# A ring of gather places that changes its size while the kernel runs

## The reference

```
qh = (x @ w_q).reshape(T, 8, 2, 128)            # 8 heads, two halves
s  = einsum('thcd,hcnd->thcn', qh, keys)        # 128 keys in each half
...                                             # top 16 of the pair sums: 16 experts of 16384 per head
gates = softmax(top_s)
act = gelu(einsum('thkd,td->thk', u[experts], x))
y   = einsum('thk,thkd->td', gates * act, v[experts])
```

## Time and profile before

| | |
|---|---|
| median of 3 runs | 4133.05 us |
| lowest and highest of them | 4130.08 and 5259.92 us |
| the profiled execution's own time | 4129.4 us |
| its span, first to last instruction | 4127.6 us |
| granted TensorE clock, mean | 0.851 |
| busy: PE, DVE, ACT, POOL | 2945.9, 3013.0, 1444.9, 1617.4 us |
| moved by DMA | 1521.92 MB, of that 1366.06 MB on Pool's queue |

### The profile page before, as it was taken

How to read it: one execution, slowest core, us unless ns; L and a number is a source line. 1 busy time by engine, 2 the same in 40 slices (tenths; PEclk the granted TensorE clock), 3 DMA queues, 4 the chain that set the end, 5 groups by cost and what they waited for, 6 DMA issues and landing times.

```text
span 4127.6 us, 32638 instructions
## 1 busy us (share of the span) xinstructions
PE 2945.9 (71%) x9247; PEld 1519.2 (37%) x9247; DVE 3013.0 (73%) x6069; ACT 1444.9 (35%) x4189; POOL 1617.4 (39%) x1309
## 2 busy tenths in 40 slices
PE   6699756875977744767868876776887787665565
PEld 2365342444532311323446323344354633222122
DVE  0406769878898846687778886978787898666666
ACT  1213323532233321335632332542475233332232
POOL 0001332334544424344433553434544354444443
PEclk8798888987999976787879998888988899888888
DMA  8143897989998999899999999999999999999998
GB/s 355 67 166 137 325 391 280 339 333 357 410 396 363 405 408 382 329 402 405 407 387 402 406 382 383 384 417 419 411 410 415 419 417 377 422 421 414 420 421 364
DMA packets 222323, 1521.92 MB, mean 369 GB/s; under 512 B 29757, under 2 KB 33537, under 8 KB 48822
## 3 DMA queue, kind: packets, MB, share of 16 engines
q0 software_dynamic: 186912, 1366.06, 81.5%
q1 hardware_dynamic: 35230, 153.77, 9.4%
HBM read 1516.49 MB, written 3.24 MB: 368 GB/s over the span
## 4 chain that ended last, share of the span: by engine, by line
DMA 31%; PE 28%; DVE 24%; issue 8%; POOL 4%; ACT 4%; DVEq 1%; SPq 1%; PEldq 1%; PEld 0%; ACTq 0%
DMA core_ring<-in_l_uv,core_experts 24%; PE sum_rows L1986 8%; DVE core_ring L1946 7%; DVE core_yv L1961 4%; POOL core_ring L1929 4%; PE sum_rows L2263 2%; PE j_in_ps L490 2%; DMA layer_slot<-in_l_uv,core_experts 1%; PE s1c_query_pq L1700 1%; DMA s0a_h_w<-in_l_peer_wq 1%; PE j_query_pq L1700 1%; DMA mod_w<-in_l_w_mod 1%; PE s1b_in_ps L490 1%; PE s0b_out_po L629 1%; DVEq L159 1%
## 5 line engine op out<-in xcount | busy, mean ns | idle before, releaser
L1929 POOL DMA_INDIRECT core_ring<-in_l_uv,core_experts x1209 | 1521.1, 1258 | 2085.0 <-PE sum_rows L1986 954.8
L1986 PE MATMUL sum_rows<-core_ring,core_diag 128*128 128x512 f32 x2820 | 1540.9, 692 | 596.7 <-ACT core_diag L1975 472.3
L1946 DVE CUSTOM_DVE_ANT_0 core_ring<-core_ring,core_hc 128x1024 f32<-128x1024 f32 x1209 | 1466.8, 1223 | 612.2 <-DMA core_ring<-in_l_uv,core_experts 433.6
L1986 PEld LDWEIGHTS sum_rows<-core_ring,core_diag 128*128 128x128 f32 x2820 | 577.7, 218 | 1482.6 <-ACT core_diag L1975 786.0
L1969 ACT ACTIVATE core_wt<-core_wt 128x1 f32<-128x1 f32 x1280 | 256.4, 200 | 1655.7 <-DVE core_wt L1946 1572.9
L1961 DVE SCALAR_TENSOR_TENSOR core_yv<-core_ring,core_wt,core_yv 128x1024 f32<-128x1024 f32 x494 | 632.8, 1281 | 17.9 <-ACT core_wt L1972 17.3
L1972 ACT ACTIVATE core_wt<-core_wt,core_gates 128x1 f32<-128x1 f32 x1280 | 376.8, 294 | 41.6
L1975 ACT ACTIVATE core_diag<-core_ident,core_wt 128x128 f32<-128x128 f32 x705 | 283.1, 402 | 23.0
L1986 PE MATMUL sum_rows<-layer_slot,layer_diag 128*128 128x512 f32 x184 | 107.7, 716 | 45.6 <-ACT layer_diag L1975 34.8
L2263 PE MATMUL sum_rows<-core_ring 128*128 128x416 f32 x320 | 117.5, 526 | 5.2 <-DVEq L159 4.1
L1946 DVE CUSTOM_DVE_ANT_0 layer_slot<-layer_slot,core_hc 128x1024 f32<-128x1024 f32 x71 | 86.9, 1224 | 40.5 <-DMA layer_slot<-in_l_uv,core_experts 30.5
(11 more groups left out here) (778 smaller groups left out, 3285.6 us busy)
## 6 DMA issues: line engine op xcount, KB each, us to landing
mod_w<-in_l_w_mod SPq DMA_DIRECT2D x16, 2048.0 KB, 11.9
core_ring<-in_l_uv,core_experts POOLq DMA_INDIRECT x1209, 11.9
core_ring<-in_l_w_mod POOLq DMA_DIRECT2D x6, 2048.0 KB, 10.1
s_mix_pr<-in_l_w_in SPq DMA_DIRECT2D x5, 1664.0 KB, 11.2
core_ring<-in_l_w_in POOLq DMA_DIRECT2D x5, 1664.0 KB, 10.5
p_h_w<-in_l_peer_wq SPq DMA_DIRECT2D x16, 512.0 KB, 4.6
s0a_h_w<-in_l_peer_wq SPq DMA_DIRECT2D x16, 512.0 KB, 12.9
s0b_h_w<-in_l_peer_wq SPq DMA_DIRECT2D x16, 512.0 KB, 8.2
```

Of the source, the lines that this page charges most:

```text
L1929: nc.gpsimd.indirect_dma_start(self.slots[r], None, core.a[f"l{layer}_uv"], bass.IndirectOffsetOnAxis(ap=self.experts[:, t, n:n + 1], axis ...
L1946: nc.vector.tensor_tensor_reduce(self.slots[r][:, 0:D], self.slots[r][:, 0:D], self.hc[:], 1.0, 0.0, ALU.mult, ALU.add, self.wt[:, r:r + 1 ...
L1986: mm = nc.tensor.matmul(self.py[:, c * 512:(c + 1) * 512], self.diags[r], self.slots[r][:, D + c * 512:D + (c + 1) * 512], start=(at == 0) ...
```

## The change

The ring's places are no longer worked out by a formula but handed out in turn from a list, `turns`, to which places can be added and from which they can be taken while the program is written out. `place(n)` pops the first of the list, notes it with its count, and puts it back at the end.

- Behind layer 0's mixers two places are opened: one for good (in a stage "late" that lasts to the end) and one in a stage "rest" that lasts over `other_experts` of layer 0 and layer 1's modulation. The second is taken out of the turns ahead of the modulation, which leaves nine.
- Behind layer 1's last attention stage two more are opened in a stage "last", which makes eleven, for what is left to gather then.
- Pool waits before the first gather into such a place until the engines' last meeting before it was opened is over (`free_from`).
- Since the places are known only when everything else is written out, both calls of `bg.gather` move to the end of `program`.
- There are twelve semaphores of each kind and twelve columns of weights (`PLACES`).

```diff
-RINGS = (RING, 9)
+PLACES = 12
...
-        self.used = [new(f"used{r}") for r in range(max(RINGS))]
+        self.used = [new(f"used{r}") for r in range(PLACES)]
...
+        self.turns, self.placed, self.times, self.free_from = list(range(RING)), [], [0] * PLACES, {}
...
-    def more_slots(self, stage):
-        for r in range(RING, RINGS[1]):
+    def open_places(self, stage, count):
+        opened = range(len(self.slots), len(self.slots) + count)
+        for r in opened:
             self.slots.append(stage.sb(f"slot{r}", [P, 2 * D])[:])
             self.diags.append(stage.sb(f"diag{r}", [P, P])[:])
+            self.free_from[r] = 4 * self.core.meetings
+            self.turns.append(r)
+        return opened
+    def close_places(self, places):
+        for r in places:
+            self.turns.remove(r)
     def place(self, n):
-        half = TILES * SLOTS
-        if n < half:
-            return n % RINGS[0], n // RINGS[0]
-        rnd, r = divmod(n - half, RINGS[1])
-        return r, rnd + (half // RINGS[0] if r < RINGS[0] else 0)
+        while len(self.placed) <= n:
+            r = self.turns.pop(0)
+            self.placed.append((r, self.times[r]))
+            self.times[r] += 1
+            self.turns.append(r)
+        return self.placed[n]
...
                     r, rnd = self.place(q * SLOTS + n)
+                    if rnd == 0 and r in self.free_from:
+                        pool.wait_ge(core.meeting, self.free_from[r])
                     pool.wait_ge(self.used[r], rnd + 1)
...
-            for r in range(max(RINGS)):
+            for r in range(PLACES):
                 dve.sem_inc(self.used[r], 1)
...
             early.load()
-            bg.gather(0)
...
-        other_experts(core, "s0b", latents[1:], 0, 1, REST_RATES)
-        with Stage(core, "mod1_c") as m:
-            modulation_stage(core, 1, "mod1", m.sb("silu", [P, DK, 32])[:], early.MOD_CHUNKS, [1, 4], 2, (2.5, PE_0, 3))
-        with Stage(core, "layer1") as last:
-            bg.more_slots(last)
-            bg.gather(1)
+        with Stage(core, "late") as late:
+            bg.open_places(late, 1)
+            with Stage(core, "rest") as rest:
+                more = bg.open_places(rest, 1)
+                other_experts(core, "s0b", latents[1:], 0, 1, REST_RATES)
+                bg.close_places(more)
+                with Stage(core, "mod1_c") as m:
+                    modulation_stage(core, 1, "mod1", m.sb("silu", [P, DK, 32])[:], early.MOD_CHUNKS, [1, 4], 2, (2.5, PE_0, 3))
             with Stage(core, "s1_att") as m:
...
-            other_experts(core, "s1c", latents[2:], 1, 7, LATENT_RATES)
-            stored = store_rows(core)
-            bg.allow(2 * TILES)
-            bg.finish(2 * TILES - 1)
...
+            with Stage(core, "last") as last:
+                bg.open_places(last, 2)
+                other_experts(core, "s1c", latents[2:], 1, 7, LATENT_RATES)
+                stored = store_rows(core)
+                bg.allow(2 * TILES)
+                bg.finish(2 * TILES - 1)
...
+        for layer in range(2):
+            bg.gather(layer)
```

More of the change, by code:

```diff
@@ L1867, in __init__ @@
         self.yv = mem.sb("yv", [P, D])
-        self.wt = mem.sb("wt", [P, max(RINGS)])
+        self.wt = mem.sb("wt", [P, PLACES])
         self.diag = mem.sb("diag", [P, RING, P])
@@ L1876, in __init__ @@
         self.gelu_done, self.wt_done, self.diag_done = new("gelu_done"), new("wt_done"), new("diag_done")
-        self.used = [new(f"used{r}") for r in range(max(RINGS))]
+        self.used = [new(f"used{r}") for r in range(PLACES)]
         self.slots = [self.ring[:, r, :] for r in range(RING)]
         self.diags = [self.diag[:, r, :] for r in range(RING)]
+        self.turns, self.placed, self.times, self.free_from = list(range(RING)), [], [0] * PLACES, {}
         self.order = new("order")
         self.gate_in = new("gate_in")
-        self.row_in = [new(f"row_in{r}") for r in range(max(RINGS))]
+        self.row_in = [new(f"row_in{r}") for r in range(PLACES)]
         self.owners, self.on_pe, self.last_add = [], places_on_pe(4), None
@@ L2496, in program, with _ @@
                 attention_stage(core, "s1c_attend", latents, [2, 3], pr, qT, kT, vc, env["h"], attention, LATENT_RATES["attend"])
-            other_experts(core, "s1c", latents[2:], 1, 7, LATENT_RATES)
-            stored = store_rows(core)
-            bg.allow(2 * TILES)
-            bg.finish(2 * TILES - 1)
-            @core.block.sync
-            def _(sp):
-                sp.wait_ge(stored, 16 * TILES)
+            with Stage(core, "last") as last:
[4 more added lines that the diff above has]
+                bg.finish(2 * TILES - 1)
+                @core.block.sync
+                def _(sp):
+                    sp.wait_ge(stored, 16 * TILES)
+        for layer in range(2):
+            bg.gather(layer)
 def store_rows(core):
```

## The result

Median 4097.52 us (4092.37 to 4099.06, 4 runs) against 4131.57 us before; the ratio is 0.9924, 95% interval 0.9912 to 0.9936. (A slow run of the kernel before, 5259.92 us, is not in the ratio.) That is 0.76% or 31 us less, where 43.6 us were forecast: clear of no change by the interval, though less than two per cent. Measured once more beside another experiment, the ratio was 0.9916 (0.9901 to 0.9931).

What follows compares the result with a forecast made beforehand. After about 900 us transfers were taken to bound the kernel, except where below 422 GB/s. Gains of 19.1, 17.4 and 7.1 us sum to 43.6 us, taken from the median 4133.05: 4089.4 us, range 4045 to 4131.

Steps and rivals of the forecast that it cites:

- The bound and the sign: After about 900 us transfers bound the kernel, except where they fall below 422 GB/s; more places save 43.6 us.
- Emission, 0: Whole program: writing the gathers out last, working out turns while building, and three more semaphores at the start cost 0.
- added waits: Pool's four waits before first gathers into new places: taken as 0, at most 2.48 us each, 10 us in all.
- Two places to 1490, 19.1 us: Gathers of about 905 to 1490 us: two more places shorten four dips by 5.0, 5.0, 5.0 and 4.1 us.
- tile boundary: Dip at 1240 to 1270 us, with Pool's 16.48 us wait: loses 14.4 us, two more places give 5.0.
- One place to 2400, 17.4 us: About 1490 to 2400 us, nine places for eight: seven dips each give one gather's 2.48 us.
- The end, 7.1 us: From 3160 us on, two more places: the dip at 3450 gives 5.0 us, that at 3800 gives 2.1.
- The bounds: Whole gain: at least 18 us by comparing stretches with eight and nine places, at most 130 us, all lost outside 2400 to 3160.
- The limit of seven gathers: Pool's descriptor memory, 1,024 bytes of a partition, holds seven gathers at most; six dips would give 15 us less, sum 29.
- Rival A: In dips foreground matmuls and DVE's order decide; only tile boundaries at 1240 and 3450 give 5.0 us each: 4123 us, chance 0.15.
- Rival B: Nearly all lost bandwidth comes back, also where few gathers are under way: 75 to 130 us saved, say 4030 us; chance 0.09.
- Rival C: In the projections foreground weights come late behind more gathers: at a quarter of 279 us, 26 us slower, 4159; chance 0.06.

Runs made afterwards that it cites:

- the first experiment: The changed kernel's new turns, waits and gathers written last, but the sizes of the kernel before (eight places, nine from gather 640): 4126.2 us, ratio 1.0001 to before.
- the fourth experiment: The kernel before's sizes (eight, then nine places) in the new way of writing out, plus two places at the end, eleven: 4123.46 us, ratio 0.9989 to before.

## Why the prediction came out right, point by point

*The bound and the sign.* Right. The stretch without a new place, 2400 to 3160, took 774 us both times; three of the four with one got shorter, by less waiting at the same busy time of DVE. The sum was too high: 43.6 us against 31. The stretches below are cut at the dot products named above and taken over all profiles with the same places in that stretch; their parts, 14, 10 and 5 us, add up to 29. Of the signs, 905 to 1470 us moved 401 GB/s, as said, and the tail stayed at 422; from 1640 to 2400 it was 391 GB/s and not 398. The range was wide, from 2 to 88 us saved, so that the time fell into it says little by itself.

*Emission, 0.* Right, by the first experiment. The added waits were not tried alone, but none shows in the changed kernel: Pool's first gathers into the new places, at 904.6, 905.8, 3147.8 and 3149.1 us, begin 0.30 us after the issue before them.

*Two places to 1490, 19.1 us.* 16 us between the two profiles; with eight places four profiles take 505 to 509 us from dot product 146 to 320, with ten four take 493 to 495: some 14 us. The term that failed is the 5.0 us for the tile boundary from 1240 to 1270: it gave nothing (14.2 us lost against 14.0). The other three terms came out near their size: ahead of the boundary, where 10.0 us were counted for two dips, 12.5 instead of 22 to 26 us are lost, and behind it 3 us less, where 4.1 were counted. The prediction took four dips as four gains; but at the boundary a new place holds a row that has landed, or one nearly so, and the queue is fed no longer for it. What decides that a row has landed by then is not shown: DVE's waits for rows just before don't tell it, since with eight places DVE still waits 4.4 us for rows from 1210 to 1220, just ahead of that dip.

*One place to 2400, 17.4 us.* Of this the two dips at the crossing, counted with 5.0 us, are gone: from dot product 320 to 430 it is 392 us before and 393 after; with eight places four profiles take 388 to 395, with nine five take 387 to 393, a scatter as large as the term. The five dips of layer 1's first stages, counted with 12.4 us, gave 6 us between the two profiles; three profiles with eight places take 592 to 596 us from 430 to 640, four with nine 582 to 586: some 10 us.

*The end, 7.1 us.* 5 us between the profiles, 4.5 by itself. The dip near 3450 shrank, but wasn't mostly gone: 360 GB/s for 330 in the fourth experiment.

*The bounds.* The place-for-place comparison, 18 us, was too low, and the bandwidth lost in all, 130 us, far too high; both ends held.

*The limit of seven gathers.* The prediction set it beside the sum, with 29 us as what would be left. The limit is there, and 29 us is near the measured 31; but that is luck, since with twice the room the kernel was some 6 us faster, not clear of noise, and not the 15 that the limit was to cost.

*Rival A*, a wait that only replaces a wait, is true of the tile boundary, of the crossing, and of 16 of the 45 us that DVE waits less for rows. The prediction had DVE's waits for rows shrink by less than the gain; they shrank by more. But A had named the tile boundaries as the two places that would give something, and one of them gave nothing. *Rival B* didn't happen. *Rival C* neither. The query loads' median time to landing, after, in the stages with ten (s0b), nine (s1b) and eleven places (s1c):

```profile
s0b_h_w<-in_l_peer_wq SPq DMA_DIRECT2D x16, 512.0 KB, 8.6
...
s1b_h_w<-in_l_peer_wq SPq DMA_DIRECT2D x16, 512.0 KB, 14.6
s1c_h_w<-in_l_peer_wq SPq DMA_DIRECT2D x16, 512.0 KB, 11.1
```

8.6, 14.6 and 11.1 us, against 8.2, 14.5 and 11.1 in the earlier trace rows. And in the kernel that never has more than three gathers under way, whose gathers land in 8.2 us:

```profile
core_ring<-in_l_uv,core_experts POOLq DMA_INDIRECT x1080, 8.2
...
s0b_h_w<-in_l_peer_wq SPq DMA_DIRECT2D x16, 512.0 KB, 8.7
...
s1b_h_w<-in_l_peer_wq SPq DMA_DIRECT2D x16, 512.0 KB, 14.0
s1c_h_w<-in_l_peer_wq SPq DMA_DIRECT2D x16, 512.0 KB, 11.0
```

8.7, 14.0 and 11.0. The last of the three decides: when the loads of s1c are issued, by issues and landings 4 gathers are under way in the median before, 6 in the changed kernel and 3 in this one. (In s0b it is 2 to 3 in all of them, so that s0b shows nothing of the depth.) Three gathers more ahead of a load would be 3 x 2.48 = 7.4 us; 11.1, 11.1 and 11.0 us show none of it. So a load doesn't wait for the gathers that were issued ahead of it. This is what the Trainium skill says on the page "DMA: Bandwidth & Descriptors" in "Queues, rings and completion order": an engine takes turns between its queues. The trace agrees, with 11.1 and 11.0 us.

## What to carry to other kernels

Not every dip of the bandwidth pays for one more buffer. In this kernel new places paid where they had more transfers under way at Pool's last issue ahead of the dip (7 and 6 instead of 5 and 4 behind their opening), and gave nothing at the tile boundary, where they held rows that had landed or nearly so. Before a dip is counted, look at that issue in the trace: how many transfers are under way, and how many buffers hold data that nobody has used yet. That this tells the worth of a dip in other kernels too is not shown.

The step that one has measured says little of the next: the eighth place gave 31 us in layer 1's first stages and the ninth some 10, but in the stretch ahead of them the eighth, ninth and tenth gave 5, 6 and 10. And filling a dip by moving work into it can come back as another dip later, so the whole time has to be measured.

## What the runs showed of the hardware that I had not expected

Gathers issued by Pool can be held up by the room for their descriptors before the ring of places is full: 1,024 bytes held seven of 1 MiB, 512 bytes three, and then Pool sits in the issue, which reads as "issue" and not as a wait. With no more than three under way the tail moved only 373 of 422 GB/s. And the time to landing of the loads on SP's queue didn't depend on the depth of Pool's queue (11.1, 11.1 and 11.0 us for the same loads with 4, 6 and 3 gathers under way).
